# Summing conditioning units 15 and 21 of a 24-unit set on VectorE instead of multiplying them on TensorE

## What is computed

```python
mod_l = split(silu(c) @ ada_w[l] + ada_b[l], 6)          # first block, also for c_ctx
x = x + mod_l[2] * token_mixer_out(zl, ...)              # hyena, fnet and mLSTM branches, gated
x = x + mod_l[5] * hier_moe(modulate(rmsnorm(x), mod_l[3], mod_l[4]))
# second block, for each of two layers:
mod = silu(c_2) @ w_ada[layer] + b_ada[layer]
```

## Time and profile before

| what | value |
|---|---|
| median of the three runs | 1872.42 us |
| the profiled execution's own time | 1873.18 us |
| its span, first to last instruction | 1871.2 us |
| TensorE (PE) busy | 1802.1 us, 96% of the span |
| VectorE (DVE) busy | 674.1 us, 36% |
| ScalarE (ACT) busy | 293.8 us, 16% |
| mean granted TensorE clock | 0.992 of full speed |
| stage of the ten passes | about 50 to 272 us of the span |

### The profile page before, as it was taken

How to read it: one execution, slowest core, us unless ns; L and a number is a source line. 1 busy time by engine, 2 the same in 40 slices (tenths; PEclk the granted TensorE clock), 3 DMA queues, 4 the chain that set the end, 5 groups by cost and what they waited for, 6 DMA issues and landing times.

```text
span 1871.2 us, 34952 instructions
## 1 busy us (share of the span) xinstructions
PE 1802.1 (96%) x15464; PEld 1004.7 (54%) x15464; DVE 674.1 (36%) x1579; ACT 293.8 (16%) x679; POOL 22.7 (1%) x37
## 2 busy tenths in 40 slices
PE   5999999999999999999999999999999999999997
PEld 2654768885444555777775555344444434344444
DVE  3766775822333464433222743101111111111023
ACT  3211121102221243100002342000000000000001
POOL 0100000000000000000000000000000000000000
PEclk9999999999999999999999999999999999999998
DMA  9968745345797322776772333999999999999995
GB/s 358 352 242 298 268 147 187 114 179 212 294 421 294 135 91 91 265 252 225 247 272 83 136 114 139 387 410 419 410 419 409 408 420 406 420 413 414 409 415 210
DMA packets 154590, 532.55 MB, mean 285 GB/s; under 512 B 9856, under 2 KB 34784, under 8 KB 120272
## 3 DMA queue, kind: packets, MB, share of 16 engines
q1 hardware_dynamic: 149360, 509.15, 70.3%
q0 software_dynamic: 3152, 14.96, 2.2%
q10 hardware_dynamic: 1920, 6.12, 0.9%
HBM read 524.29 MB, written 9.04 MB: 285 GB/s over the span
## 4 chain that ended last, share of the span: by engine, by line
PE 89%; DVE 5%; DMA 2%; DVEq 1%; ACT 1%; issue 1%; SPq 0%; ACTq 0%
PE ps L1412 24%; PE ps L1424 12%; PE ps L1225 8%; PE ps L1582 8%; PE ps L1088 4%; PE ps L1207 4%; PE ps L1237 4%; PE ps L893 4%; PE ps L1283 3%; PE ps L1103 2%; PE ps L1316 2%; PE ps L758 1%; DMA ring<-in_ada_w 1%; PE ps L700 1%; PE ps L1275 1%
## 5 line engine op out<-in xcount | busy, mean ns | idle before, releaser
L1412 PE MATMUL ps<-ring,arena 128*32 128x512 f32 (+1 forms) x4608 | 459.1, 557 | 0.0
L1412 PEld LDWEIGHTS ps<-ring,arena 128*32 128x32 f32 x4608 | 149.3, 110 | 293.7 <-issue 287.0
L1424 PE MATMUL ps<-ring,arena 128*32 128x256 f32 x4224 | 232.2, 379 | 0.0
L1424 PEld LDWEIGHTS ps<-ring,arena 128*32 128x32 f32 x4224 | 139.7, 110 | 96.5 <-issue 12.3
L3059 DVE TENSOR_TENSOR arena<-arena,ps 128x256 f32<-128x256 f32 (+1 forms) x72 | 27.0, 375 | 390.3 <-ACT arena L2092 390.3
L1582 PE MATMUL ps<-ring,hT 128*128 128x512 f32 (+1 forms) x384 | 154.9, 554 | 1.5 <-DVE hT L2341 1.5
L1225 PE MATMUL ps<-hT,ring 128*128 128x256 f32 x704 | 153.8, 379 | 0.7 <-DVE hT L2341 0.7
L1225 PEld LDWEIGHTS ps<-hT,ring 128*128 128x128 f32 x704 | 133.8, 190 | 23.2 <-issue 5.7
L1582 PEld LDWEIGHTS ps<-ring,hT 128*128 128x128 f32 x384 | 69.2, 190 | 68.8 <-issue 66.9
L893 PE MATMUL ps<-hT,ring 128*128 128x256 f32 x384 | 88.1, 383 | 0.8 <-DVE hT L2341 0.8
L2092 ACT ACTIVATE arena<-ps 128x256 f32<-128x256 f32 (+1 forms) x72 | 21.2, 367 | 422.0 <-PE ps L1412 422.0
(11 more groups left out here) (430 smaller groups left out, 1662.2 us busy)
## 6 DMA issues: line engine op xcount, KB each, us to landing
ring<-in_gate_up SPq DMA_DIRECT2D x160, 1024.0 KB, 14.4
ring<-in_down SPq DMA_DIRECT2D x104, 1024.0 KB, 16.0
ring<-in_gate_up_last SPq DMA_DIRECT2D x64, 768.0 KB, 14.4
ring<-in_w_ada SPq DMA_DIRECT2D x48, 768.0 KB, 6.0
ring<-in_w_in SPq DMA_DIRECT2D x36, 768.0 KB, 6.9
ring<-in_ada_w SPq DMA_DIRECT2D x24, 768.0 KB, 8.2
ring<-in_w_ada SPq DMA_DIRECT2D x24, 512.0 KB, 7.0
ring<-in_w_in SPq DMA_DIRECT2D x12, 1024.0 KB, 7.4
```

The costliest lines, as they stand in the source:

```text
L1412: last = mm(ps[32 * q:32 * q + 32, base + t_, 0:2 * n], src[:, k, 32 * t_:32 * t_ + 32], w[:, q], start=k == 0, stop=k == KD - 1)
L1424: last = mm(ps[32 * q:32 * q + 32, bank + t_ // 2, (t_ % 2) * 256:(t_ % 2 + 1) * 256], rows[:, t_, o:o + 32], cells[:, cell, r * D + q * 2 ...
```

## The change

`SUMMED` gets the units 15 and 21. VectorE runs `ada_sum` of unit 15 between line 2528 and `o_in(1)`, and `ada_sum` of unit 21 at j = 4 of the head loop. `17 + j` gives 17, 19 and 21 for j = 0, 2 and 4, so 17 and 19 stay where they were.

```diff
-SUMMED = (10, 11, 12, 13, 14, 17, 19)
+SUMMED = (10, 11, 12, 13, 14, 15, 17, 19, 21)
@@ VectorE, behind the two scans @@
             scans(gm, gi, ALU.max, gi)
             v.tensor_tensor(gf, gB, gm, ALU.add).then_inc(sem("ml_ready"), 1)
+            ada_sum(*ADA_UNITS[15])
             o_in(1)
             dve.wait_ge(sem("ml_cols_mm"), 1)
@@ VectorE, in the loop over j @@
                 if j:
                     head_out(j - 1)
-                if j in (0, 2):
-                    ada_sum(*ADA_UNITS[19 if j else 17])
+                if j in (0, 2, 4):
+                    ada_sum(*ADA_UNITS[17 + j])
```

## The result

The changed kernel took 1884.57 us (median of 5 runs, 1882.07 to 1886.24) against 1873.07 us for the kernel before (5 runs, 1871.66 to 1877.19). The ratio is 1.006, with a 95% interval of 1.0044 to 1.0076, so it is slower by 0.44% to 0.76%, or 11.5 us between the medians. The forecast was 1881.3 us and its range ended at 1884.5. The direction and the mechanism held; the size came out 3.3 us above the forecast, 0.07 us above the upper end.

The account below looks back on a forecast made before the run. TensorE was taken as the bound, with 89% of the chain of waits. Terms 6.6 + 2.2 + 0.1 = 8.9 us on the median 1872.42 gave 1881.3 us, range 1878.3 to 1884.5.

Parts of the forecast that it names:

- Unit 15, the wait, +6.6: Before line 952 in pass 5, TensorE waits for VectorE's sum behind line 2528, then does tiny matmuls: 6.6 us later.
- Unit 15, what is removed buys nothing: Dropping 1.84 us of TensorE matmuls in pass 5 gains nothing, because TensorE already waited there until 174.10 us.
- The clock, +2.2: Behind about 9.0 us of TensorE idle before line 952, the clock falls to 1.2 GHz, costing 2.2 us (0 to 3.9).
- Unit 21, +0.1: At j = 4 of the heads, VectorE's idle 1.60 and 4.33 us swallow the sum: +0.1 us, between 0 and +0.5.
- The loads, 0: Loads of weights and units released later, around passes 5 to 9, still land before they are wanted: cost 0.
- (a): Rival: the clock does not fall, or recovers at once, so only the wait stays: 1879.1 us; chance 0.10.
- (b): Rival: the clock stays low longer behind the wait, 3.9 us in place of 2.2: 1883.0 us; chance 0.15.
- (c): Rival: the kernel gets faster because matmul time on TensorE is what counts: -3.0 us, 1869.5 us; chance 0.02.
- (d): Rival: some wait between 181 and 272 us takes the delay up: no change, 1873.5 us; chance 0.04.
- (e): Rival: the weights of pass 7 land after TensorE wants them, another 3 us on top: 1884.3 us; chance 0.04.
- The test named for being wrong: Prediction wrong if line 952 directly follows 2528, 952 to 1116 grows other than about 2 us, or DMA ends passes 6-9 waits.

## Why the prediction was right, and where it was short

- **Unit 15, the wait, +6.6.** Right: 6.84 us from line 2528 to line 952 against 0.05, and 6.72 us in B-C in both kernels that have it. Unit 15 alone gave the whole loss, and moving its sum took most of it away.
- **Unit 15, what is removed buys nothing.** Right, and more than that: the 1.84 us had kept TensorE at work in front of the gates. Without them the wait is 2.99 us even where the sum is elsewhere.
- **The clock, +2.2.** The mechanism was right and the term too small. In C-D it cost 3.49 us in the changed kernel's profile and 2.10 us with unit 15 alone. The term was taken from falls that cost 1.7 to 2.6 us, but here the clock stayed low for longer: for some 8.3 us of TensorE's work in the first profile and 5.4 in the second. (These are estimates. A clock of 0.81 over 182 to 186 us puts the rise at 183.5, and 0.62 over 183 to 187 puts it at 186.0; line 700 began at 175.25 and 180.59.) Whether the rest of the difference is the clock too is less clear. Over the runs the mean clock fell from 0.9942 (the 35 runs of the kernel before) to 0.9906 (5 runs), which at 1.4 us for 0.001 would be 5.0 us. But about 5 us of the low clock, from 170 to 175.25, lie in the idle time, where they lower the mean by 0.0014 and cost nothing. That leaves an estimated 3.1 us, and with the 6.7 us of the wait 9.8 of the 11.5 measured. The 1.7 us left are no more than the 1.8 by which the kernel before differed from itself. In the changed kernel's profile the wait for the merge's first load was 4.49 us, the clock was low behind it, and line 1088 took 9.68 us in place of 7.17. That is not the change's own doing, as far as the profiles show: the same line took 9.99 to 10.10 us with unit 21 alone (the second time), the wait filled, unit 14 back and unit 10 back. Whether the change makes it more frequent is open.
- **Unit 21, +0.1.** Right in the profile: 8.60 us against 8.52 on VectorE, and 0.04 to 0.07 us between lines 952 and 1116 when it is alone. Over the whole kernel its medians were 2.6 and 2.7 us up, which is not explained; the changed kernel, which has unit 21 too, lost no more than unit 15 alone.
- **The loads, 0.** Right for passes 6 to 9: no load ends a wait there. Behind them E-F grew from 6.06 to 8.19 us in the changed profile. It is between 6.1 and 7.4 in the others, whichever units are summed. From the issue of the merge's loads to line 1088 it took 10.4 us before (270.12 to 280.50), 11.8 us in the changed kernel (275.85 to 287.63), and as much, 11.7 us, with only unit 18 summed in addition (270.06 to 281.80). So most of it can be scatter of the load; that was not tested.
- **The rivals.** (a) fell: the clock was at 0.50 from 170 to 182 us. (b) is near what the changed kernel's profile showed behind the wait (3.5 us, 3.9 forecast), and its 1883.0 us would have been the nearer number; unit 15 alone, with 2.1 us, is at the forecast's own 2.2. (c) and (d) fell. For (e) the weights of pass 7 were there in time.
- **The test named for being wrong** was a distance from line 952 to line 1116 that grows by other than about 2 us. It grew by 3.3, from 100.34 to 103.66 us, and by 2.2, to 102.55, with unit 15 alone. The term that was mis-sized is the clock's: 2.2 us in the sum, 3.49 and 2.10 measured behind the wait.

## What to carry to other kernels

In this case, moving work off the busiest engine could pay only where the chain runs through that engine, and where the other engine's idle time takes the work before anyone waits for it. Here one unit placed behind the scans cost 7 us of waiting, and the same sort of unit placed in VectorE's idle time cost under 0.1 us in its stretch. Before work is taken from TensorE in front of a wait, ask whether it was filling that wait. The clock behind the wait cost another 2.1 to 3.5 us here. Balancing both engines so that neither waits (units 10 and 14 back, unit 18 over) gained 0.4%, although none of the three moves showed a gain alone.

## What the runs showed of the hardware that was not expected

The clock falls behind shorter waits than the prediction took into account, and not every time. Behind the same 0.94 us of wait at the gates, followed by the tiny gate matmuls and another wait of 0.28 us, it stayed at 1.00 in both profiles of the kernel before and fell with unit 18 summed, which cost 1.7 us. Behind the same 2.90 us at A it was low in nine profiles and stayed up in two (the changed kernel and the kernel before, run again). Such falls, at 1.7 us or so each, go with executions of one kernel that differ by several us: 1868.33 us at a mean clock of 0.997 and 1878.49 at 0.992 for the kernel before. A difference of 2 us between medians of 12 runs was therefore not a result here. The distances between fixed points in the profiles did show effects of that size.
